# Big matmuls of a three-pass fp32 kernel take turns between two PSUM banks

## The chip, the cores and the metric

The kernel runs on one core of one Trainium2 chip. The metric is the device time of one execution in microseconds (us); lower is better. The kernel before takes 2294.41 us, the median of 3 runs (2293.33 to 2296.01).

## What is computed

Two transformer-like blocks follow each other on 256 tokens of width 2048, all in fp32:

```
hybrid_layer:  h = rmsnorm(x, g_mix) @ w_in                 # 2048 x 5728 columns in nine parts
               y_ssd = state-space scan of (xbc, dt), gated by z
               y_att = attention over the top 64 keys by an index score
               x = x + concat(y_ssd, y_att) @ w_out         # 2048 x 2048
               u = rmsnorm(x, g_mlp) @ w_up                 # 2048 x 8192
               x = x + square(relu(u)) @ w_down             # 8192 x 2048
second block:  h = rmsnorm(x, g0) @ fox_w_in                # 2048 x (3 * 2048 + 16)
               h = forget-gate attention, 16 heads, @ fox_w_out
               x = x + rmsnorm(h, g1)
               h = square(relu(rmsnorm(x, g2) @ mlp_w1)) @ mlp_w2
               x = x + rmsnorm(h, g3)
```

## The kernel before

Nearly all of the work is products of 256 tokens with weight matrices that come from HBM once. A matrix is worked through in **panels** of 2048 x 512 weights: 95 of them. A panel has four **chunks** `j` of 512 x 512 weights (1 MB), and a chunk has four **k-tiles** `kk` of 128 rows.

An fp32 product is made of three matmuls of a narrower float type. Each operand is split in a high and a low part: SyncE loads a chunk into `raw`, ScalarE rounds it into `wh` (L501), VectorE subtracts and writes `wl` (L942). Activations are kept split in the same way (`XH`, `XL`, or `hh`, `hl` for the hidden layer). TensorE adds high x high, high x low and low x high into PSUM.

There are two forms of panel, and in both a panel's result lies in two PSUM banks of 128 x 512 fp32, `acc[o_par][0]` and `acc[o_par][1]` (banks 0 and 1 for even panels' outputs, banks 2 and 3 for odd ones; the other four banks serve small side work):

- `rows`: tokens are the stationary operand (128 of them), weights are moving (512 columns). Token tile `t` has bank `t`. A k-tile is 2 token tiles x 3 matmuls (L1705, L1706, L1707), a chunk is 24 matmuls.
- `cols`: weights are stationary (128 features), tokens are moving (256 columns). Feature tile `f` of four has a half of bank `f // 2`. A k-tile is 4 feature tiles x 3 matmuls (L1720, L1722, L1723), a chunk is 48 matmuls.

```
for kk in range(4):
    for t in tokens:              # rows: three matmuls into one bank, then the other
        o = acc[o_par][t][:, :]
...
for kk in range(4):
    for f in range(4):            # cols: six matmuls into one bank, then the other
        o = acc[o_par][f // 2][:, TOK * (f % 2):TOK * (f % 2 + 1)]
```

The order of the work on TensorE is written out by hand: `panel` and `first_panel` call one of the two forms for each chunk, and between chunks a table (`MIX_AT`, `FOX_AT`) puts side work into the row: transposes, index scores, attention heads. A chunk waits once, at its start, for `lo_ready` (its `wl`). A panel waits once, at its start, in `acc_wait`, for both of its banks to be read out (`acc_freed`). The last matmul of a chunk raises `chunk_used`; SyncE's next load of the same buffer, and ScalarE and VectorE's reading of a finished panel, wait for that. The end of the kernel has another order: for the last two chunks `rows` is called with one token tile at a time (`tokens` of `[0]` for both chunks, then of `[1]` for both), so that the first tile can be finished while the second is computed. There 24 successive matmuls write one bank, and then 24 the other.

Of the kernel before, what the change touches and what calls it, by code (L numbers as in the profile page):

```python
# [18 lines left out]
P = 128  # L19
TOK = 256  # L20
# [41 lines left out]
def hybrid_then_fox(nc, x, g_mix, w_in, conv_w, conv_b, dt_bias, a_log, d_skip, g_ssd, g_q, g_k,  # L62
# [3 lines left out]
    with ctx:  # L66
# [3 lines left out]
        def sb(name, shape, dt=F32):  # L70
            return ctx.enter_context(nc.sbuf_tensor(name, shape, dt))
# [3 lines left out]
        XH = sb("XH", [P, KT, TOK], F32R)  # L75
        XL = sb("XL", [P, KT, TOK], F32R)
        wh = sb("wh", [P, 4, 4, 512], F32R)
# [29 lines left out]
        raw, wl = T["raw"], T["wl"]  # L107
# [58 lines left out]
        acc = [[bank[0], bank[1]], [bank[2], bank[3]]]  # L166
# [1522 lines left out]
        def _(pe):  # L1689
# [7 lines left out]
            def rows(b, j, o_par, first, last, k0, h=XH, l=XL, tokens=range(NT), used=chunk_used):  # L1697

                pe.wait_ge(lo_ready, 4 * b + j + 1)
                for kk in range(4):  # L1700
                    for t in tokens:
                        o = acc[o_par][t][:, :]
                        sh, sl = (z[:, k0 + kk, t * P:(t + 1) * P] for z in (h, l))
                        mh, ml = wh[:, j, kk, :], wl[:, j, kk, :]
                        pe.matmul(o, sh, mh, start=first and kk == 0, stop=False)  # L1705
                        pe.matmul(o, sh, ml, start=False, stop=False)  # L1706
                        mm = pe.matmul(o, sl, mh, start=False, stop=last and kk == 3)  # L1707
                if used is not None:
                    mm.then_inc(used, 1)

            def cols(b, j, o_par, first, last, k0):


                pe.wait_ge(lo_ready, 4 * b + j + 1)
                for kk in range(4):
                    for f in range(4):
                        o = acc[o_par][f // 2][:, TOK * (f % 2):TOK * (f % 2 + 1)]
                        sh, sl = (z[:, j, kk, f * P:(f + 1) * P] for z in (wh, wl))
                        mh, ml = XH[:, k0 + kk, :], XL[:, k0 + kk, :]
                        pe.matmul(o, sh, mh, start=first and kk == 0 and f % 2 == 0, stop=False,  # L1720
                                  skip_group_check=True)
                        pe.matmul(o, sh, ml, start=False, stop=False, skip_group_check=True)  # L1722
                        mm = pe.matmul(o, sl, mh, start=False, stop=last and kk == 3, skip_group_check=True)  # L1723
                mm.then_inc(chunk_used, 1)

            def turn_quarter(m, q):
# [30 lines left out]
            def panel(form, b, o, plan={}, slot=0):  # L1757
                acc_wait(o)
                for j in range(4):
                    if form is cols:  # L1760
                        cols(b, j, o % 2, j == 0, j == 3, 4 * j)
                    else:
                        rows(b, j, o % 2, j == 0, j == 3, 4 * j)
                    side_work(plan, slot + j)

            def mlp(m, b0, o0, u0):
                for half in range(2):
                    b, o, u = b0 + half * B_HALF, o0 + half * O_HALF, u0 + half * UP
                    if half == 0:
                        first_panel(cols, m, b, o)  # L1770
                    else:
                        panel(cols, b, o)
                    with pe.Fori(0, UP // 2 - 1) as i:
                        for s in (1, 2):
                            for k in range(2):
                                pe.wait_ge(acc_freed[(o + s) % 2][k], i + (o + s) // 2)
                            for j in range(4):
                                cols(b + 2 * i + s, j, (o + s) % 2, j == 0, j == 3, 4 * j)
                    panel(cols, b + UP - 1, o + UP - 1)
                    for n in range(DOWN):  # L1780
                        on = o + UP + n
                        acc_wait(on)
                        for j in range(8):
                            if n == 0:

                                pe.wait_ge(hl_ready, 2 * (u + j) + 4)
                            if m == 3 and half == 1 and n == DOWN - 1 and j > 5:
                                continue
                            rows(b + UP + 2 * n + j // 4, j % 4, on % 2, j == 0, j == 7, 4 * j, hh, hl)
                            if half == 1 and m == 1 and n > 0 and j == 3:  # L1790
                                turn_quarter(2, n - 1)
                if m == 3:

                    rows(B_END - 1, 2, on % 2, False, False, 24, hh, hl, [0], None)
                    rows(B_END - 1, 3, on % 2, False, True, 28, hh, hl, [0], first_tokens)
                    rows(B_END - 1, 2, on % 2, False, False, 24, hh, hl, [1])
                    rows(B_END - 1, 3, on % 2, False, True, 28, hh, hl, [1])
# [236 lines left out]
```

## Time and profile before

| | |
|---|---|
| median of 3 runs | 2294.41 us |
| profiled execution | 2293.16 us |
| its span | 2291.4 us |
| TensorE matmul busy | 2261.6 us (99%), 14211 instructions |
| TensorE weight load busy | 2024.1 us (88%) |
| VectorE busy | 1208.5 us (53%) |
| ScalarE busy | 946.4 us (41%) |
| DMA engines, mean | 55.7% by the weights' queue, 180 GB/s |
| mean granted TensorE clock | 0.998 |

The span is the time from the first to the last instruction of the profiled execution; 1.8 us lie around it. Matmuls are pipelined: one begins before the one ahead of it has ended, so the time of one is longer than its share of TensorE. What a matmul costs is the distance from its start to the next one's start, which the timeline gives, in steps of 0.01 us. Busy time above is the union of overlapping matmuls.

### The profile page before, as it was taken

Reading aid. Unit: us, or ns where it says so; the run is one execution under the profiler, and the core shown is the slowest. Engines: PE = TensorE matmul, PEld = TensorE weight load, DVE = VectorE, ACT = ScalarE, POOL = GpSimd, SP = SyncE. Lnnn points to the kernel's source line nnn. Section 1 sums busy time; section 2 is a strip of 40 time slices with the busy share of each in tenths; the row PEclk is TensorE's granted clock in tenths of the full one; section 3 lists DMA queues with packets and bytes.
Section 4 is the critical chain, followed back from the end, with each engine's and each line's share of the span. In section 5 each row is a group of like instructions: output and inputs, shape, how many; then the busy total and the mean of one; then the engine's idle time right before and its main releaser. Section 6 shows DMA issues by size and latency. Waiting matters only on the chain.

```text
span 2291.4 us, 32313 instructions
## 1 busy us (share of the span) xinstructions
PE 2261.6 (99%) x14211; PEld 2024.1 (88%) x14211; DVE 1208.5 (53%) x1167; ACT 946.4 (41%) x901; POOL 12.4 (1%) x34
## 2 busy tenths in 40 slices
PE   7999999999999999999999999999999999999998
PEld 7988778999988899988899987888998888999886
DVE  5688665545444354544455444555555443545444
ACT  5453564444433343434334434434435333434332
POOL 1000000000000000000000000000000000000000
PEclk9999999999999999999999999999999999999999
DMA  8445435666555666555555454555665556665554
GB/s 259 152 157 166 156 129 190 196 184 183 184 190 193 186 184 183 184 184 184 185 184 183 148 165 155 176 186 171 184 184 192 185 184 188 185 184 189 190 184 147
DMA packets 210908, 412.12 MB, mean 180 GB/s; under 512 B 12804, under 2 KB 12896, under 8 KB 210160
## 3 DMA queue, kind: packets, MB, share of 16 engines
q1 hardware_dynamic: 210368, 409.89, 55.7%
q8 instruction: 88, 1.44, 0.3%
q0 software_dynamic: 432, 0.62, 0.2%
q14 instruction: 20, 0.16, 0.0%
HBM read 408.39 MB, written 2.10 MB: 179 GB/s over the span
## 4 chain that ended last, share of the span: by engine, by line
PE 98%; DVE 1%; ACT 1%; DMA 0%; issue 0%; DVEq 0%; SPq 0%; ACTq 0%
PE bank L1705 16%; PE bank L1706 16%; PE bank L1707 16%; PE bank L1720 15%; PE bank L1723 15%; PE bank L1722 15%; PE bank L1803 1%; PE bank L1735 1%; PE bank L1828 0%; PE bank L1837 0%; PE bank L1922 0%; PE bank L1896 0%; PE bank L1815 0%; PE bank L1807 0%; PE bank L1829 0%; DMA G<-in_g_mix_dram 0%
## 5 line engine op out<-in xcount | busy, mean ns | idle before, releaser
L942 DVE TENSOR_TENSOR wl<-raw,wh 128x2048 fp32r<-128x2048 f32 x380 | 870.3, 2291 | 647.3 <-ACT wh L501 645.2
L501 ACT ACTIVATE wh<-raw 128x2048 fp32r<-128x2048 f32 x380 | 726.7, 1913 | 724.8 <-DMA raw<-in_mlp_w_dram 265.0
L1720 PE MATMUL bank<-XH,wh 128*128 128x256 f32 x2880 | 817.7, 284 | 0.2 <-issue 0.2
L1723 PE MATMUL bank<-XH,wl 128*128 128x256 f32 x2880 | 812.7, 282 | 0.0
L1722 PE MATMUL bank<-XL,wh 128*128 128x256 f32 x2880 | 810.3, 281 | 0.0
L1722 PEld LDWEIGHTS bank<-XL,wh 128*128 128x128 f32 x2880 | 547.2, 190 | 0.6 <-issue 0.5
L1720 PEld LDWEIGHTS bank<-XH,wh 128*128 128x128 f32 x2880 | 543.7, 189 | 3.7 <-issue 2.2
L1723 PEld LDWEIGHTS bank<-XH,wl 128*128 128x128 f32 x2880 | 542.8, 188 | 0.0
L1707 PE MATMUL bank<-wh,hl 128*128 128x512 f32 x1024 | 404.5, 395 | 0.0
L1706 PE MATMUL bank<-wl,hh 128*128 128x512 f32 x1024 | 404.4, 395 | 0.0
L1705 PE MATMUL bank<-wh,hh 128*128 128x512 f32 x1024 | 402.2, 393 | 0.0
L1706 PEld LDWEIGHTS bank<-wl,hh 128*128 128x128 f32 x1024 | 191.9, 187 | 47.0
L1705 PE MATMUL bank<-wh,XH 128*128 128x512 f32 x576 | 231.9, 403 | 1.3 <-DVE XL L950 1.3
L1705 PEld LDWEIGHTS bank<-wh,hh 128*128 128x128 f32 x1024 | 192.0, 188 | 45.5
L1707 PEld LDWEIGHTS bank<-wh,hl 128*128 128x128 f32 x1024 | 192.2, 188 | 44.1
L1706 PE MATMUL bank<-wl,XH 128*128 128x512 f32 x576 | 227.2, 394 | 0.0
L1707 PE MATMUL bank<-wh,XL 128*128 128x512 f32 x576 | 225.1, 391 | 0.0
L1098 DVE TENSOR_TENSOR RB<-RB 128x512 f32<-128x512 f32 x64 | 44.1, 689 | 244.8 <-ACT RB L594 244.8
L594 ACT ACTIVATE RB<-bank 128x512 f32<-128x512 f32 x64 | 38.1, 595 | 303.2 <-PE bank L1723 303.2
L1705 PEld LDWEIGHTS bank<-wh,XH 128*128 128x128 f32 x576 | 108.5, 188 | 26.1 <-issue 2.0
L1707 PEld LDWEIGHTS bank<-wh,XL 128*128 128x128 f32 x576 | 108.3, 188 | 26.0
L1706 PEld LDWEIGHTS bank<-wl,XH 128*128 128x128 f32 x576 | 108.0, 188 | 22.7 <-issue 0.5
(310 smaller groups left out, 819.7 us busy)
## 6 DMA issues: line engine op xcount, KB each, us to landing
raw<-in_mlp_w_dram SPq DMA_DIRECT2D x128, 1024.0 KB, 5.4
raw<-in_w_up_dram SPq DMA_DIRECT2D x64, 1024.0 KB, 5.5
raw<-in_w_down_dram SPq DMA_DIRECT2D x64, 1024.0 KB, 5.0
raw<-in_fox_w_in_dram SPq DMA_DIRECT2D x48, 1024.0 KB, 5.1
raw<-in_w_in_dram SPq DMA_DIRECT2D x44, 1024.0 KB, 5.0
raw<-in_w_out_dram SPq DMA_DIRECT2D x16, 1024.0 KB, 5.1
raw<-in_fox_w_out_dram SPq DMA_DIRECT2D x16, 1024.0 KB, 5.1
G<-in_norm_g_dram SPq DMA_DIRECT2D x4, 1024.0 KB, 5.9
```

The source lines that it names most:

```text
L501: act.activation(wh[:, j, :, :], raw[:, j, :, :], ACT.Copy).then_inc(hi_ready, 1)
L594: act.activation(RB[:, k, :], acc[o_par][k][:, :], ACT.Relu)\
L942: dve.tensor_tensor(wl[:, j, :, :], raw[:, j, :, :], wh[:, j, :, :].bitcast(F32), ALU.subtract)\
L1098: dve.tensor_tensor(RB[:, k, :], RB[:, k, :], RB[:, k, :], ALU.mult).then_inc(sq_ready, 1)
L1705: pe.matmul(o, sh, mh, start=first and kk == 0, stop=False)
L1706: pe.matmul(o, sh, ml, start=False, stop=False)
L1707: mm = pe.matmul(o, sl, mh, start=False, stop=last and kk == 3)
L1720: pe.matmul(o, sh, mh, start=first and kk == 0 and f % 2 == 0, stop=False, skip_group_check=True)
L1722: pe.matmul(o, sh, ml, start=False, stop=False, skip_group_check=True)
L1723: mm = pe.matmul(o, sl, mh, start=False, stop=last and kk == 3, skip_group_check=True)
L1735: mm = pe.transpose(bk[:, i * P:(i + 1) * P], src[:, t, k * P:(k + 1) * P], ident[:, :])
L1803: mm = pe.matmul(bk[:, ctr(t)], q[:, t * P:(t + 1) * P], k[:, 0:(t + 1) * P], start=True, stop=not a)
```

## The change

In `rows`, the loop over token tiles moves inside the loop over the three products, so successive matmuls write bank 0, 1, 0, 1. In `cols`, the four feature tiles are taken as two pairs `(0, 2)` and `(1, 3)`, each with one tile in either bank, and the pair is the innermost loop. For one output tile the three products and the k-tiles keep their order. `start`, which clears a bank's accumulation, stays on the first matmul that a panel makes in each bank.

```diff
                 for kk in range(4):
-                    for t in tokens:
-                        o = acc[o_par][t][:, :]
-                        sh, sl = (z[:, k0 + kk, t * P:(t + 1) * P] for z in (h, l))
-                        mh, ml = wh[:, j, kk, :], wl[:, j, kk, :]
-                        pe.matmul(o, sh, mh, start=first and kk == 0, stop=False)
-                        pe.matmul(o, sh, ml, start=False, stop=False)
-                        mm = pe.matmul(o, sl, mh, start=False, stop=last and kk == 3)
+                    mh, ml = wh[:, j, kk, :], wl[:, j, kk, :]
+                    for x, m in ((h, mh), (h, ml), (l, mh)):
+                        for t in tokens:
+                            mm = pe.matmul(acc[o_par][t][:, :], x[:, k0 + kk, t * P:(t + 1) * P], m,
+                                           start=first and kk == 0 and x is h and m is mh,
+                                           stop=last and kk == 3 and x is l)
...
                 for kk in range(4):
-                    for f in range(4):
-                        o = acc[o_par][f // 2][:, TOK * (f % 2):TOK * (f % 2 + 1)]
-                        sh, sl = (z[:, j, kk, f * P:(f + 1) * P] for z in (wh, wl))
-                        mh, ml = XH[:, k0 + kk, :], XL[:, k0 + kk, :]
-                        pe.matmul(o, sh, mh, start=first and kk == 0 and f % 2 == 0, stop=False,
-                                  skip_group_check=True)
-                        pe.matmul(o, sh, ml, start=False, stop=False, skip_group_check=True)
-                        mm = pe.matmul(o, sl, mh, start=False, stop=last and kk == 3, skip_group_check=True)
+                    mh, ml = XH[:, k0 + kk, :], XL[:, k0 + kk, :]
+                    for half in range(2):
+                        for w, m in ((wh, mh), (wh, ml), (wl, mh)):
+                            for f in (half, half + 2):
+                                mm = pe.matmul(acc[o_par][f // 2][:, TOK * (f % 2):TOK * (f % 2 + 1)],
+                                               w[:, j, kk, f * P:(f + 1) * P], m,
+                                               start=first and kk == 0 and half == 0 and w is wh and m is mh,
+                                               stop=last and kk == 3 and w is wl, skip_group_check=True)
```

How the order on TensorE moves is seen at two places. The first is a k-tile of the first `cols` chunk (out <- moving operand, stationary operand, and the moving shape). Before:

```order
L1720 MATMUL bank0<-XH,wh 128x256
L1722 MATMUL bank0<-XL,wh 128x256
L1723 MATMUL bank0<-XH,wl_50 128x256
L1720 MATMUL bank0<-XH,wh 128x256
L1722 MATMUL bank0<-XL,wh 128x256
L1723 MATMUL bank0<-XH,wl_50 128x256
L1720 MATMUL bank1<-XH,wh 128x256
L1722 MATMUL bank1<-XL,wh 128x256
L1723 MATMUL bank1<-XH,wl_50 128x256
```

Now, on TensorE at the same place:

```order
L1719 MATMUL bank0<-XH,wh 128x256
L1719 MATMUL bank1<-XH,wh 128x256
L1719 MATMUL bank0<-XL,wh 128x256
L1719 MATMUL bank1<-XL,wh 128x256
L1719 MATMUL bank0<-XH,wl_50 128x256
L1719 MATMUL bank1<-XH,wl_50 128x256
L1719 MATMUL bank0<-XH,wh 128x256
```

Where the bank changed after every sixth matmul, it changes after each. The second place is the start of a `rows` chunk of the first MLP's second layer. Before:

```order
L1705 MATMUL bank2<-wh,hh_97 128x512
L1706 MATMUL bank2<-wl_50,hh_97 128x512
L1707 MATMUL bank2<-wh,hl_98 128x512
L1705 MATMUL bank3<-wh,hh_97 128x512
L1706 MATMUL bank3<-wl_50,hh_97 128x512
L1707 MATMUL bank3<-wh,hl_98 128x512
L1705 MATMUL bank2<-wh,hh_97 128x512
```

Now, on TensorE at the same place:

```order
L1704 MATMUL bank2<-wh,hh_97 128x512
L1704 MATMUL bank3<-wh,hh_97 128x512
L1704 MATMUL bank2<-wl_50,hh_97 128x512
L1704 MATMUL bank3<-wl_50,hh_97 128x512
L1704 MATMUL bank2<-wh,hl_98 128x512
L1704 MATMUL bank3<-wh,hl_98 128x512
L1704 MATMUL bank2<-wh,hh_97 128x512
```

Where the bank changed after every third matmul, it changes after each. The orders of VectorE, ScalarE and SyncE are the same before and after, and TensorE issues as many matmuls. Where `rows` is called with one token tile, nothing moves.

## Rows read from the trace of the kernel before

**Rows 1.** The page: busy time of the engines, granted TensorE clock in 40 slices

```profile
PE 2261.6 (99%) x14211; PEld 2024.1 (88%) x14211; DVE 1208.5 (53%) x1167; ACT 946.4 (41%) x901; POOL 12.4 (1%) x34
...
PEclk9999999999999999999999999999999999999999
```

**Rows 2.** The page: the chain that ended last, by engine and by line

```profile
PE 98%; DVE 1%; ACT 1%; DMA 0%; issue 0%; DVEq 0%; SPq 0%; ACTq 0%
PE bank L1705 16%; PE bank L1706 16%; PE bank L1707 16%; PE bank L1720 15%; PE bank L1723 15%; PE bank L1722 15%; PE bank L1803 1%; PE bank L1735 1%; PE bank L1828 0%; PE bank L1837 0%; PE bank L1922 0%; PE bank L1896 0%; PE bank L1815 0%; PE bank L1807 0%; PE bank L1829 0%; DMA G<-in_g_mix_dram 0%
```

**Rows 3.** Waits of TensorE: total us, times, longest

```profile
PE bank L1735 <- DVE XN L974: 14.0, 2, 8.0
PE bank L1735 <- DVE HG L1643: 4.7, 1, 4.7
```

**Rows 4.** Groups of matmuls by shape: busy us, mean ns | idle before

```profile
L1720 PE MATMUL bank<-XH,wh 128*128 128x256 f32 x2880 | 817.7, 284 | 0.2 <-issue 0.2
L1723 PE MATMUL bank<-XH,wl 128*128 128x256 f32 x2880 | 812.7, 282 | 0.0
L1722 PE MATMUL bank<-XL,wh 128*128 128x256 f32 x2880 | 810.3, 281 | 0.0
...
L1706 PE MATMUL bank<-wl,hh 128*128 128x512 f32 x1024 | 404.4, 395 | 0.0
L1705 PE MATMUL bank<-wh,hh 128*128 128x512 f32 x1024 | 402.2, 393 | 0.0
L1705 PE MATMUL bank<-wh,XH 128*128 128x512 f32 x576 | 231.9, 403 | 1.3 <-DVE XL L950 1.3
```

**Rows 5.** Timeline of a cols chunk: start us, us; matmuls 1, 3, 4, 6, 7, 48

```profile
595.43 0.28 PE L1720 MATMUL bank<-XH,wh 128*128 128x256 f32 x1
...
595.67 0.28 PE L1723 MATMUL bank<-XH,wl 128*128 128x256 f32 x1
595.79 0.29 PE L1720 MATMUL bank<-XH,wh 128*128 128x256 f32 x1
...
596.03 0.28 PE L1723 MATMUL bank<-XH,wl 128*128 128x256 f32 x1
596.14 0.28 PE L1720 MATMUL bank<-XH,wh 128*128 128x256 f32 x1
...
601.03 0.28 PE L1723 MATMUL bank<-XH,wl 128*128 128x256 f32 x1
```

**Rows 6.** Timeline, 48 rows matmuls that change bank every third: first, last

```profile
2260.85 0.39 PE L1705 MATMUL bank<-wh,hh 128*128 128x512 f32 x1
...
2271.76 0.39 PE L1707 MATMUL bank<-wh,hl 128*128 128x512 f32 x1
```

**Rows 7.** Timeline, the kernel's last 48 matmuls, 24 in each bank: first, last

```profile
2272.00 0.39 PE L1705 MATMUL bank<-wh,hh 128*128 128x512 f32 x1
...
2282.91 0.40 PE L1707 MATMUL bank<-wh,hl 128*128 128x512 f32 x1
```

**Rows 8.** Timeline, 45 narrow matmuls of side work in one bank: first, last

```profile
66.14 0.28 PE L1859 MATMUL bank<-XH,NHm 128*96 128x256 f32 x1
...
71.28 0.28 PE L1861 MATMUL bank<-XH,NLm 128*96 128x256 f32 x1
```

**Rows 9.** Weight loads of cols: busy us, mean ns | idle before

```profile
L1722 PEld LDWEIGHTS bank<-XL,wh 128*128 128x128 f32 x2880 | 547.2, 190 | 0.6 <-issue 0.5
L1720 PEld LDWEIGHTS bank<-XH,wh 128*128 128x128 f32 x2880 | 543.7, 189 | 3.7 <-issue 2.2
```

**Rows 10.** Stretches after a wait of TensorE; the eighth column is the granted clock

```profile
1555.00:1556.00 1.00, 0.76 (x4) 0.76 (x5) 1.00 (x3) 0.00 (x0) 0.00 (x0) 0.50 0.28 107
1556.00:1559.50 3.50, 3.29 (x19) 3.08 (x18) 1.89 (x3) 2.85 (x3) 0.00 (x0) 0.67 0.00 0
```

**Rows 11.** Timeline, the program's second and sixth cols matmul

```profile
17.95 0.41 PE L1722 MATMUL bank<-XL,wh 128*128 128x256 f32 x1
...
18.81 0.35 PE L1723 MATMUL bank<-XH,wl 128*128 128x256 f32 x1
```

## The prediction

> **What bounds the kernel now.** The order of reading is: busy time, the chain, TensorE's waits, the groups, and then the timeline, because the groups can't price this change. TensorE is busy for 99% of the span, VectorE for 53% and ScalarE for 41%, at full granted clock in all slices [rows 1]. The chain that ended last is TensorE for 98%, and six lines, the three matmuls of `rows` and the three of `cols`, make 93 of these points [rows 2]. TensorE's own waits come to some 19 us in its two main rows [rows 3], both before transposes that follow a normalization, where no big matmul stands. So the time is the number of big matmuls times the distance between their starts, and a change of their order counts in full or not at all: nothing hides it, and nothing else is in line to take over soon.
>
> The groups give 281 to 284 ns for a matmul of 256 columns and 393 to 403 ns for one of 512 [rows 4]. The reader must not take these as prices: a matmul begins before the one ahead of it has ended. The distance of starts is the price. In a chunk of `cols`, 48 matmuls span 595.43 to 601.03, which is 5.60 us over 47 steps, 119.1 ns a step [rows 5]. In `rows`, 48 matmuls span 2260.85 to 2271.76, 10.91 us over 47 steps, 232.1 ns [rows 6]. There are 3 x 2880 = 8640 of the first kind [rows 4], and 3 x (1024 + 576) = 4800 of the second. 8640 x 0.1191 + 4800 x 0.2321 = 1029 + 1114 = 2143 us, 93.5% of the span of 2291.4 us, which agrees with the chain.
>
> **The change, part by part.** No instruction comes or goes on TensorE, and VectorE, ScalarE and SyncE keep their order. What changes is which matmul follows which.
>
> *Steps to another bank.* `cols` has 8640 / 48 = 180 chunks. Before, 8 steps in 48 go to the other bank, now all do: 40 x 180 = 7200 new ones. `rows` has 4800 / 24 = 200 chunks; two at the end are worked one bank at a time and stay. Before, 8 steps in 24 change bank, now all do: 16 x 198 = 3168 new ones. Together 10,368 steps inside a bank become steps between banks. What is one worth? The kernel before holds both kinds at the same shape. The 48 matmuls of [rows 6] change bank after every third one, 15 times in 47 steps. The 48 that follow, the kernel's last, write 24 times one bank and 24 times the other, one change in 47 steps, with the same three products and the same shapes, and they too span 10.91 us, from 2272.00 to 2282.91 [rows 7]. Fourteen steps inside a bank in place of steps between banks cost 0.00 us. So a step between banks is worth nothing, and I put this term at **0**. The timeline is rounded to 0.01 us, so the bound on either side is 0.01 / 14 = 0.7 ns a step, and 10,368 x 0.7 ns = **7.3 us either way**. For `cols` the price is carried over from `rows`; what its own rows say agrees as far as they go: the step from the third to the fourth matmul, in one bank, is 0.12 us, and that from the sixth to the seventh, between banks, 0.11 us, one rounding step apart [rows 5]. And 45 matmuls of 256 columns that all write one bank are 5.14 us over 44 steps, 116.8 ns [rows 8]: a bit shorter than in `cols`, where every sixth step changes bank. They have 96 stationary columns where `cols` has 128, so this is a near row, not the same shape; but a penalty for staying in a bank would have made them the longer ones.
>
> A rule of the Trainium skill speaks for a gain, and this trace weighs against its use. The page "TensorE: Matmul & The Clock Gate", in "Wait — 56ns, not 53.3ns?", has warm matmuls start every N / 2.4 GHz + 2.5 ns, which is 109 ns at 256 columns and 216 ns at 512; here they are 10 and 16 ns slower. If all that were the price of staying in a bank, the change would bring 7200 x 10 + 3168 x 16 ns = 123 us, an estimate by that page, and the faster rival below would end at 2171 us. The comparison of [rows 6] and [rows 7] says that the excess, whatever it is, doesn't hang on the bank.
>
> *Steps with the same weights.* Before, the second matmul of each three has the stationary operand of the first; now none has, except in the one-tile calls. TensorE loads the weights anew in either case: there are as many loads as matmuls [rows 1], and in `cols` the load for L1722, whose weights are already in, takes 190 ns against 189 ns for L1720 [rows 9]. Nothing is skipped today, so nothing is lost: **0**. Both loads are longer than a step of 119 ns, so they overlap one another, as before. The bound is in the rivals.
>
> *Steps with the same moving operand.* Before, one step in four of `cols` and one in six of `rows` keeps it, now about half do. The step from L1723 to L1720 keeps it and takes 0.12 and 0.11 us in [rows 5], the chunk's mean is 0.119: **0**, within what the rounding shows.
>
> *Waits.* A panel waits for both banks before its first matmul, so that the second bank is written sooner (second matmul in place of fourth or seventh) costs nothing. A chunk's last matmul still raises `chunk_used`, so the loads into `raw`, and the reading of a finished panel, start as before. Bank 0 gets its last product next to the end rather than three or six matmuls ahead, but nobody reads it sooner than bank 1. No engine has a new wait. If TensorE did get faster, ScalarE and VectorE, at 41 and 53%, would still follow.
>
> The sum is 0. The profiled execution took 2293.16 us, and would take 2293.2 us. The median of the runs stands 1.25 us above it, so the forecast is **2294.4 us**.
>
> **The rivals.** 0.2%, or 4.6 us, is about what a measurement of this kernel can tell from no change.
>
> *Faster: staying in a bank costs something that the end of the kernel doesn't show.* From 256 to 512 columns a step grows by 232.1 - 119.1 = 113.0 ns; taken off the 119.1 ns, that leaves 6.1 ns that don't depend on the columns. Were these the bank's turnaround, 10,368 x 6.1 ns = 63 us would go: 2231 us. It decides from 0.45 ns a step on. For it: the constant exists, and nothing in the trace names its cause. Against it: [rows 7] would then be 14 x 6.1 = 85 ns longer than [rows 6], and they are equal to 10 ns; the narrow matmuls in one bank would be longer, and are not. Chance 0.08, most of it for a small gain in `cols`, where the like comparison is missing.
>
> *Slower: the weights.* If a load of unchanged weights does save something, at the place where L1722 and L1706 follow L1720 and L1705, the new order loses it in 2880 + 1584 = 4464 steps. In the groups L1722 is 3 ns shorter than L1720 [rows 4]. 4464 x 3 ns = 13 us: 2308 us. It decides from 1.0 ns a step. Against it: in `rows` L1706, on unchanged weights, is 2 ns longer than L1705, L1723 on new weights is only 1 ns longer than L1722, and L1720's mean holds the first matmuls of the program, at 0.4 us and more. Chance 0.04.
>
> *Slower: the clock.* After the wait of 4.7 us the granted clock was 0.50, the level of 1.2 GHz, and 0.67 on average over the next 3.5 us [rows 10]; together some 3.3 us at the lower level. The slowest even stretch of `cols` steps is at the program's start, 0.86 us over four steps, 215 ns [rows 11], 96 ns over the usual. A fall of 3.3 us holds 15 such steps and costs 1.5 us; three are needed to be seen, and one in each of the 45 panels of `cols` would cost 68 us: 2362 us. It takes gaps that TensorE doesn't have between big matmuls, and the change makes none. Chance 0.02. The Trainium skill has it as a danger of just this kind of order, in the same page under "A second HAM failure mode: psum-queue depth-cycling": cycling through banks left the engine with small pauses between groups, and its clock went up and down. This trace disagrees as far as it goes: `rows` changes bank at every third matmul, and the clock stays at 9 tenths or more in every slice [rows 1].
>
> *The change doesn't do what it says* can be left out: the order above shows the banks taking turns.
>
> **How the numbers follow.** No change has 0.86, faster 0.08, slower 0.06 (0.04 + 0.02). The range takes the bounds of the first term, 2294.4 - 7.3 and 2294.4 + 7.3, and so 2287 to 2302 us; the runs' own scatter (2293.3 to 2296.0) lies inside. The rivals' own numbers are outside it, their small versions inside.
>
> **What would show it.** In the profile after, a chunk of `cols` should again span 5.60 us over 47 steps and one of `rows` 232.1 ns a step, now with the banks alternating; the kernel's last 48 matmuls, which are not touched, should again span 10.91 us, like those ahead of them. The weight loads stay at 189 ns, and the waits before the transposes at 14 and 4.7 us. Wrong would be a step of `rows` of 228 ns (two thirds of the steps lose 6.1 ns) with 232 ns left at the end (the faster rival), steps 1 ns or more longer with the loads unchanged in number (the weights), or slices with a clock below 9 (the clock).

## The result: slower by 0.3%, and the profile after

The changed kernel takes 2301.39 us, the median of 10 runs (2297.95 to 2304.01), against 2294.54 us for the kernel before (10 runs, 2292.99 to 2296.66). The ratio is 1.0029, with a 95% interval of 1.0021 to 1.0038. The profiled execution took 2303.71 us and its span is 2302.0 us, 10.6 us over that of before. The median lies inside the range that was forecast; "no change" was wrong.

The page of the kernel after, the lines that answer to [rows 1] and [rows 2]:

```profile
PE 2272.4 (99%) x14211; PEld 2033.6 (88%) x14211; DVE 1208.3 (52%) x1167; ACT 946.6 (41%) x901; POOL 12.4 (1%) x34
...
PEclk9999999999999999999999999999999999999999
...
PE 98%; DVE 1%; ACT 1%; DMA 0%; issue 0%; DVEq 0%; SPq 0%; ACTq 0%
```

Everything is as it was but TensorE's busy time, which is 10.8 us longer for matmuls and 9.5 us longer for weight loads. The same number of each runs; the waits before the transposes are those of [rows 3]:

```profile
PE bank L1734 <- DVE XN L974: 14.1, 2, 8.0
PE bank L1734 <- DVE HG L1643: 4.7, 1, 4.7
```

So the steps between matmuls got longer. A step that is 1 ns longer can't be read from rows rounded to 10 ns, but it can be counted: in a fixed stretch that holds nothing but `cols` matmuls, a slower pace shows as fewer of them. Each of the two MLPs computes its hidden layer in two halves, each with 32 chunks of `cols` and then `rows` on `hh`; so there are four such stretches. Windows of 160 us in them, of the kernel before; the columns are the stretch, its length, TensorE's busy time and number of matmuls, granted clock, DMA share and GB/s:

```profile
435.00:595.00 160.00, 160.00 (x1346) 1.00 0.61 184
797.00:957.00 160.00, 160.00 (x1347) 1.00 0.61 184
1583.00:1743.00 160.00, 160.00 (x1346) 1.00 0.61 184
1935.00:2095.00 160.00, 160.00 (x1346) 1.00 0.61 184
```

The same windows of the kernel after:

```profile
435.00:595.00 160.00, 160.00 (x1335) 1.00 0.60 182
797.00:957.00 160.00, 160.00 (x1336) 1.00 0.61 184
1583.00:1743.00 160.00, 160.00 (x1336) 1.00 0.61 182
1935.00:2095.00 160.00, 160.00 (x1336) 1.00 0.61 182
```

Ten or eleven in 1346 are missing, 0.8%, at full clock: a step takes 119.9 ns in place of 119.06 ns. (The window counts one or two matmuls that reach in from its edges.) The loss isn't spread evenly. The timeline after shows pairs of matmuls there, with 0.25 us from the pair on `wl` to the next and 0.23 us from that to the third:

```profile
820.30 0.40 PE L1719 MATMUL bank<-XH,wl 128*128 128x256 f32 x2
820.55 0.40 PE L1719 MATMUL bank<-XH,wh 128*128 128x256 f32 x2
820.78 0.40 PE L1719 MATMUL bank<-XL,wh 128*128 128x256 f32 x2
```

By the starts in nanoseconds, averaged over the second half's chunks, the step from the last matmul on `wl` to the first on the next pair of tiles takes 124 ns and the other five 118 to 121 ns, and the weight load for that first matmul takes 195 ns. Before, the mean step is at most 120 ns in every place of the order and the mean load at most 190 ns. Over the whole kernel this load's group now has a mean of 192 ns, where [rows 9] has 189:

```profile
L1719 PEld LDWEIGHTS bank<-XH,wh 128*128 128x128 f32 x2880 | 450.1, 192 | 4.3 <-issue 2.6
```

A sum over the starts of all matmuls, kind by kind and against before, says where the 10.5 us between the first and the last matmul are: `cols` +7.6 us, `rows` on `XH` and `XL` +3.0 us, `rows` on `hh` and `hl` +0.1 us, side work -0.2 us. Of these, 1.0 and 1.5 us lie in single long steps. The 1.0 us in `cols` are mostly at the program's start, where after has 12 steps at some 213 ns and before 4. The 1.5 us in `rows` on `XH` are one fall of the clock, to be seen in the windows of after and then of before:

```profile
321.20:324.40 3.20, 3.20 (x8) 0.50 0.00 0
```

```profile
321.20:324.40 3.20, 3.20 (x15) 1.00 0.00 0
```

Eight matmuls run there at half clock in place of 15, just after a wait of 1.3 us. Such a fall isn't part of the pace: it comes and goes between executions of one kernel (e8 has it and e2, the same kernel, doesn't), and the kernel before has in its own runs levels 1.5 us apart (near 2293.1, 2294.6 and 2296.2), which would fit such falls, though no trace of its higher levels was kept. But the change may make it more frequent. Besides after it is in five of the profiles below (e4, e7, e8, e11, e12), and all six have the change's rhythm of weight loads in `cols` (e8 with the old `rows`); three more profiles with that rhythm and the eight without it have no fall there. It is a part of why one profile says 10.6 us and the medians 6.9. What is left in this profile as the change's own is a pace: some 6.6 us in `cols` and 1.5 us in `rows` on `XH`.

### The profile page after: what moved, and what is told of

Read it like the earlier page. It is cut to its first block, busy times and chain, and to the rows that moved or that the text cites. A ratio compares the mean times of both kernels' runs of the same rounds, so it can differ in the third digit from the quotient of the medians.

```text
span 2302.0 us, 32313 instructions
## 1 busy us (share of the span) xinstructions
PE 2272.4 (99%) x14211; PEld 2033.6 (88%) x14211; DVE 1208.3 (52%) x1167; ACT 946.6 (41%) x901; POOL 12.4 (1%) x34
## 4 chain that ended last, share of the span: by engine, by line
PE 98%; DVE 1%; ACT 1%; DMA 0%; issue 0%; DVEq 0%; SPq 0%; ACTq 0%
PE bank L1704 48%; PE bank L1719 45%; PE bank L1802 1%; PE bank L1734 1%; PE bank L1827 0%; PE bank L1836 0%; PE bank L1921 0%; PE bank L1895 0%; PE bank L1814 0%; PE bank L1806 0%; PE bank L1828 0%; DMA G<-in_g_mix_dram 0%; PE bank L1843 0%; DVE X L1684 0%; PE bank L1859 0%; PE bank L1858 0%
## 5 line engine op out<-in xcount | busy, mean ns | idle before, releaser
L1719 PE MATMUL bank<-XH,wh 128*128 128x256 f32 x2880 | 581.5, 284 | 0.0
L1719 PE MATMUL bank<-XH,wl 128*128 128x256 f32 x2880 | 581.4, 285 | 0.0
L1719 PE MATMUL bank<-XL,wh 128*128 128x256 f32 x2880 | 577.5, 282 | 0.0
L1719 PEld LDWEIGHTS bank<-XH,wh 128*128 128x128 f32 x2880 | 450.1, 192 | 4.3 <-issue 2.6
L1719 PEld LDWEIGHTS bank<-XL,wh 128*128 128x128 f32 x2880 | 442.2, 189 | 0.0
L1719 PEld LDWEIGHTS bank<-XH,wl 128*128 128x128 f32 x2880 | 441.6, 188 | 0.0
L1704 PE MATMUL bank<-wh,hl 128*128 128x512 f32 x1024 | 323.8, 396 | 0.0
L1704 PE MATMUL bank<-wl,hh 128*128 128x512 f32 x1024 | 322.3, 395 | 0.0
L1704 PE MATMUL bank<-wh,hh 128*128 128x512 f32 x1024 | 320.4, 393 | 0.0
L1704 PE MATMUL bank<-wh,XH 128*128 128x512 f32 x576 | 184.3, 401 | 1.3 <-DVE XL L950 1.3
```

Of the source, the lines that this page charges most:

```text
L1704: mm = pe.matmul(acc[o_par][t][:, :], x[:, k0 + kk, t * P:(t + 1) * P], m, start=first and kk == 0 and x is h and m is mh, stop=last and k ...
L1719: mm = pe.matmul(acc[o_par][f // 2][:, TOK * (f % 2):TOK * (f % 2 + 1)], w[:, j, kk, f * P:(f + 1) * P], m, start=first and kk == 0 and ha ...
```

## The experiments

Two theories at first: the new **order of operands** costs the time, or the **turns between banks** do. In `cols` the runs with other orders than the change's use one loop, whose two expressions give for each of the 12 matmuls of a k-tile the feature tile `f` and the product `n`, and, where it is not that tile's own, the output tile `g`; `rows` has the like for 6 matmuls:

```python
for p in range(12):
    f, n = ...                  # before: p // 3, p % 3
    g = f                       # the change: p // 6 + 2 * (p % 2), p % 6 // 2
    w, m = ((wh, mh), (wh, ml), (wl, mh))[n]
    mm = pe.matmul(acc[o_par][g // 2][:, TOK * (g % 2):TOK * (g % 2 + 1)], w[:, j, kk, f * P:(f + 1) * P], m, ...)
```

**e1, e2: half of the change each.** The new `rows` with the old `cols`, and the reverse.

> The change in rows alone, cols as before. The trace of the changed kernel has its rows chunks of the MLP layers at the old pace and its cols chunks slower. Theory 'weights' (in cols, and only there, the weight load that opens a new pair of tiles is slower because of the new order of stationary and moving operands): no change, 2294 to 2296 us, rows steps 232 ns. Rival 'banks' (taking turns between banks costs something everywhere): +2 to +3 us, since rows have 3168 of the 10368 new bank steps.

> The change in cols alone, rows as before. Theory 'weights': the whole loss is here: cols steps of 119.9 instead of 119.05 ns, 8640 x 0.95 ns = +8 us, about 2302 us. Rival 'banks': about two thirds of the loss, +5 us.

e1 took 2297.26 us, ratio 1.0009 (0.9999 to 1.0018); e2 took 2297.31 us, ratio 1.0008 (0.9999 to 1.0018). The windows of e1, and then of e2:

```profile
797.00:957.00 160.00, 160.00 (x1346) 1.00 0.61 184
```

```profile
435.00:595.00 160.00, 160.00 (x1348) 1.00 0.61 184
797.00:957.00 160.00, 160.00 (x1348) 1.00 0.61 184
```

Both intervals reach down to no change, so the medians alone say little; the traces say more. e1's 2.3 us over the kernel before of its own round is what the theory 'banks' expected, but its trace has 1.46 us of it in `rows` on `XH`, nothing in `rows` on `hh`, which take 2016 of the 3168 new turns between banks, and its `cols` keep their pace. e2 fits neither theory. It has the new `cols`, and in the MLPs they are *faster* than before: 1348 in a window, 118.9 ns a step. Only 30 of its 180 chunks, in the projections, are at 119.9. (A chunk's pace is taken from the starts of its 7th and its 48th matmul.) On balance the pace costs e2 nothing: its `cols` steps, the single long ones left out, are 119.04 ns on average, as before. So the two halves don't add: the new `cols` order has two paces, and something about `rows` decides between them.

**e3, e4: banks alone, operands alone.** In `rows` and `cols`, a product no longer goes to the output tile of its own operands, so neither kernel computes the result; they are there for their time.

```diff
 # e3
+f, n = p // 3, p % 3                          # operands as before
+g = p // 6 + 2 * (p % 2)                      # banks as in the change
 # e4
+f, n = p // 6 + 2 * (p % 2), p % 6 // 2       # operands as in the change
+g = p // 3                                    # banks as before
```

> Operands in the order of the kernel before (the three products of a tile one after the other), but the matmuls write the banks in the order of the changed kernel, 0, 1, 0, 1; so products are added into the wrong tile, and the time alone is meant. Theory 'weights': time of the kernel before, 2294 to 2296 us, cols steps 119.05 ns, weight loads 189 ns at every position. Rival 'banks': the time of the changed kernel, about 2302 us, with one step in six of 123 to 124 ns.

> The opposite: operands in the order of the changed kernel, banks written in the order of the kernel before (three or six matmuls in a row to one bank), so products again go to the wrong tile. Theory 'weights': the time of the changed kernel, about 2302 us, with a load of 194 ns and a step of 123 to 124 ns at every sixth cols matmul. Rival 'banks': 2294 to 2296 us.

e3 took 2293.86 us, ratio 0.9998 (0.9989 to 1.0008); e4 took 2299.98 us, ratio 1.0021 (1.0011 to 1.0031). e3, then e4:

```profile
797.00:957.00 160.00, 160.00 (x1346) 1.00 0.61 184
...
1935.00:2095.00 160.00, 160.00 (x1347) 1.00 0.61 184
```

```profile
435.00:595.00 160.00, 160.00 (x1347) 1.00 0.60 183
797.00:957.00 160.00, 160.00 (x1336) 1.00 0.60 182
1583.00:1743.00 160.00, 160.00 (x1348) 1.00 0.61 184
1935.00:2095.00 160.00, 160.00 (x1336) 1.00 0.61 184
```

This settles the banks. With the turns of the change and the operands of before, the sum over the starts differs from before by 0.0 us in `rows`, and `cols` are 0.1 us shorter. The loss comes with the operands, and in e4 both paces stand side by side: two of the four halves at 1347 to 1348, two at 1336; 98 chunks are slow. In e4's second half the two signs of its expectation are there, every sixth step at 124 ns and the load for the next matmul at 195 ns; in e3's they are not.

**e5, e6: moving operands alone, stationary operands alone.** Banks as before. Stationary and moving tiles no longer belong together, so these two don't compute the result either.

```diff
 # e5
+f, n = p // 3, p % 3                          # stationary, as before
+f2, n2 = p // 6 + 2 * (p % 2), p % 6 // 2     # moving, as in the change
 # e6: the two exchanged
```

> Stationary operands and banks in the order of the kernel before, moving operands in the order of the changed kernel (each read twice in a row), in rows and cols; the pairs don't match, so products are wrong, and the time alone is meant. The profiles show that operand order, not bank order, carries the loss, that a cols chunk now runs at one of two paces, 118.9 or 119.9 ns a step, and that rows on XH and XL lose 0.8 ns a step. Theory 'weight loads' (the order in which stationary tiles are loaded decides): 2294 to 2296 us, cols at the old mixed pace of 119.05, no chunk at 119.9. Rival 'moving' (reading the same moving tile twice in a row decides): about 2300 us, many chunks at 119.9.

> The other half: stationary operands in the order of the changed kernel (two tiles in turn), moving operands and banks as before; products again wrong, the time alone is meant. Theory 'weight loads': about 2300 us, many cols chunks at 119.9 ns a step and rows on XH at +0.8 ns. Rival 'moving': 2294 to 2296 us.

e5 took 2295.78 us, ratio 1.0002 (0.9992 to 1.0011), e6 2296.24 us, ratio 1.0005 (0.9995 to 1.0014). The medians tell nothing apart; the traces do. Windows of e5, then of e6:

```profile
797.00:957.00 160.00, 160.00 (x1346) 1.00 0.61 184
```

```profile
797.00:957.00 160.00, 160.00 (x1349) 1.00 0.61 185
```

The stationary order puts `cols` on the two paces (e6: 118.9 ns in the MLPs, 30 chunks at 119.9 ns), the moving order doesn't (e5: no chunk at 119.9). But the moving order costs something in `rows` on `XH`. A run of 336 such matmuls without a break, its first and last rows, of before (to its end 1472.66 to 1550.58, 77.92 us):

```profile
1472.66 0.48 PE L1705 MATMUL bank<-wh,XH 128*128 128x512 f32 x1
...
1550.18 0.40 PE L1707 MATMUL bank<-wh,XL 128*128 128x512 f32 x1
```

of after (1479.88 to 1558.15, 78.27 us; the last row holds two):

```profile
1479.88 0.48 PE L1704 MATMUL bank<-wh,XH 128*128 128x512 f32 x1
...
1557.52 0.63 PE L1704 MATMUL bank<-wh,XL 128*128 128x512 f32 x2
```

and of e5 (1473.69 to 1551.97, 78.28 us):

```profile
1473.69 0.48 PE L1709 MATMUL bank<-wh,XH 128*128 128x512 f32 x1
...
1551.57 0.40 PE L1709 MATMUL bank<-wh,XL 128*128 128x512 f32 x1
```

Reading each moving tile twice in a row costs 0.35 us in 336 steps, 1 ns each; e6, without it, is at 77.92 us again, and over all `rows` on `XH` e5 loses 1.47 us, e6 0.0 us. So 'weight loads' held for `cols`, and 'moving' for `rows` on `XH`.

**e7, e8: the change, and its cols alone, once more.** For a second profile of each.

> The changed kernel itself once more, for a second profile. If the pace of a chunk is chosen by chance at the entry and then kept, the number of cols chunks at 119.9 ns differs from the 158 of 180 of the first profile, and the time with it, by 0.05 us a chunk. If it is fixed by the program, the same chunks are slow again.

> The change in cols alone once more: its first profile had 30 of 180 cols chunks at 119.9 ns and ran 2293.66 us, while its median was 2297.31. By chance at the entry: a number of slow chunks between 30 and 158, in step with the time. Fixed by the program: 30 again, with a time near 2294 us.

e7 took 2301.47 us and e8 2296.23 us (one execution each). The windows of e7:

```profile
435.00:595.00 160.00, 160.00 (x1347) 1.00 0.61 183
797.00:957.00 160.00, 160.00 (x1335) 1.00 0.60 182
1583.00:1743.00 160.00, 160.00 (x1348) 1.00 0.61 184
1935.00:2095.00 160.00, 160.00 (x1336) 1.00 0.61 184
```

The first profile had all four halves slow (158 chunks), this one the second and the fourth (98 chunks, the same as in e4). e8 has the 30 slow chunks of e2. So the pace of a half is settled within its first chunks and then kept, and it is partly chance. It isn't always the first chunk's: in the first profile the first half had three chunks at 118.9 ns before 29 at 119.9, and the third half one before 31. The first and third halves, which follow the norm's transposes, went either way; the others, which follow `rows` on `hh`, were slow in both profiles of the change and fast in both of its `cols` alone. They were fast in e6 too, where `rows` have the new stationary and the old moving order, and slow in e4, where they have both new. A half at the slow pace costs 32 x 48 x 1.0 ns = 1.5 us over the fast one.

**e9 to e12: what in the order does it, and what picks the pace.** The new `rows` are in e9 to e11. New theories for the order: the loads never repeat a tile; they jump by two tiles; two tiles take turns.

```diff
 # e9, neighbours (0, 1), (2, 3) in turn
+f, n = 2 * (p // 6) + p % 2, p % 6 // 2
 # e10, one tile at a time, wh wl wh
+f, n = p // 3, (0, 2, 1)[p % 3]
 # e11, wh0 wh0 wh2 wh2 wl0 wl2
+f, n = p // 6 + 2 * (0, 0, 1, 1, 0, 1)[p % 6], (0, 1, 0, 1, 2, 2)[p % 6]
 # e12, the new cols; rows in the new order only on hh and hl
+if h is XH:
+    ...
```

> The changed rows; in cols pairs of neighbouring tiles (0, 1) and (2, 3), both in one bank, in place of (0, 2) and (1, 3), products outside as in the change. Computes the reference. The runs so far show that the order of stationary tiles makes cols chunks lock to 118.9 or 119.9 ns a step. Theory 'no repeat' (it matters that no weight tile is loaded twice in a row, not which tile comes between): chunks at 118.9 and 119.9 again, many of them slow, 2299 to 2302 us. Rival 'distance' (it matters that the loads jump by two tiles, 1 KB in a partition): the old mixed pace of 119.06, about 2297 us with the 1.5 us of the changed rows.

> The changed rows; in cols one tile at a time as before, but its products in the order wh*XH, wl*XH, wh*XL, so that no weight tile is loaded twice in a row and no other tile comes between. Computes the reference up to the order of the sums. Theory 'no repeat': chunks lock to 118.9 or 119.9, 2299 to 2302 us. Rival 'alternation' (two feature tiles in turn is what matters): the old mixed pace of 119.06, about 2297 us.

> The changed rows; in cols pairs (0, 2) and (1, 3), but wh of a tile is loaded twice in a row as before: wh0 wh0 wh2 wh2 wl0 wl2. Computes the reference. Theory 'no repeat': old mixed pace of 119.06, about 2297 us. Rival 'alternation': chunks at 118.9 and 119.9, 2299 to 2302 us.

> The changed cols, and the changed rows only where they run on hh and hl (the MLPs' second layers); rows on XH and XL as before. The changed cols alone had 30 of 180 chunks at 119.9 in both profiles, the whole change 158 and about 98, although the rows on hh cost the same in either order. Theory 'entry' (the rows that a stretch of cols chunks follows decide at which of two paces it locks): the MLPs' cols chunks are slow in part as in the whole change, 80 or more slow chunks and 2297 to 2300 us. Rival 'XH rows' (the earlier rows on XH, or their 1.4 us, make the difference): 30 slow chunks, about 2296 us.

| run | median us | ratio to before | slow chunks of 180 |
|---|---|---|---|
| e9 | 2299.73 | 1.0020 (1.0010 to 1.0030) | 99 |
| e10 | 2295.46 | 1.0005 (0.9996 to 1.0015) | 0 |
| e11 | 2302.12 | 1.0027 (1.0017 to 1.0037) | 129 |
| e12 | 2299.50 | 1.0022 (1.0013 to 1.0032) | 128 |

Two windows each of e9, e10, e11, and then all four of e12:

```profile
797.00:957.00 160.00, 160.00 (x1336) 1.00 0.60 182
...
1935.00:2095.00 160.00, 160.00 (x1336) 1.00 0.61 182
```

```profile
797.00:957.00 160.00, 160.00 (x1346) 1.00 0.61 186
...
1935.00:2095.00 160.00, 160.00 (x1346) 1.00 0.61 184
```

```profile
797.00:957.00 160.00, 160.00 (x1336) 1.00 0.60 182
...
1935.00:2095.00 160.00, 160.00 (x1335) 1.00 0.60 181
```

```profile
435.00:595.00 160.00, 160.00 (x1347) 1.00 0.61 183
797.00:957.00 160.00, 160.00 (x1336) 1.00 0.60 182
1583.00:1743.00 160.00, 160.00 (x1335) 1.00 0.61 184
1935.00:2095.00 160.00, 160.00 (x1335) 1.00 0.61 184
```

e9 refutes the jump. e10 refutes "no repeat", which was also the mechanism of my rival on the weights: no tile is loaded twice in a row, and the pace is the old one; and e11 keeps the repeats and is as slow as the change. Alternation is left, or something that e9 and e11 share with the change and e10 doesn't: four loads from `wh` and then two from `wl`. e12 confirms the entry: `rows` on `hh` in the new order, themselves no slower, turn the halves that follow them, the second and the fourth, from e2's 1348 to 1336 and 1335; the third, which goes by chance, is slow here too.

**e13, e14: turns of two tiles, or the rhythm of the two weight buffers.** Again with the new `rows`.

```diff
 # e13: wh0 wh2 wl0 wh0 wh2 wl2
+f, n = p // 6 + 2 * (0, 1, 0, 0, 1, 1)[p % 6], (0, 0, 2, 1, 1, 2)[p % 6]
 # e14: each product over all four tiles
+f, n = (0, 2, 1, 3)[p % 4], p // 4
```

> The changed rows; in cols tiles and banks mostly take turns, but the loads come from the two weight buffers in the old rhythm of high, high, low: (wh0,XH) (wh2,XH) (wl0,XH) (wh0,XL) (wh2,XL) (wl2,XH). Computes the reference up to the order of the sums. So far every order with four loads from wh and then two from wl has chunks locked at 118.9 and 119.9 ns, and the orders with a rhythm of three have none. Theory 'rhythm of the buffers': no chunk at 119.9, pace 119.0 to 119.1, about 2296 us. Rival 'alternation' (two tiles in turn): 98 to 158 chunks at 119.9, 2299 to 2302 us.

> The changed rows; in cols each product runs over all four tiles, banks in turn: eight loads from wh, then four from wl. Computes the reference. Theory 'rhythm of the buffers': chunks locked again at some pace of their own (a rhythm of twelve), not the mixed pace of 119.06; if like the rhythm of six, 2297 to 2302 us. Rival 'alternation': here tiles never come back within a product and no two are in turn, so the mixed pace of 119.06 and about 2296 us.

e13 took 2295.45 us, ratio 1.0006 (0.9996 to 1.0016), e14 2294.76 us, ratio 1.0001 (0.9992 to 1.0011). e13, then e14:

```profile
797.00:957.00 160.00, 160.00 (x1347) 1.00 0.60 184
```

```profile
797.00:957.00 160.00, 160.00 (x1348) 1.00 0.61 184
...
1935.00:2095.00 160.00, 160.00 (x1348) 1.00 0.61 184
```

e13 mostly keeps the turns and has the old rhythm of high, high, low, and the old pace, with no slow chunk: the rhythm decides, not the turns. What it is about the rhythm isn't separated: its length of six, or that loads from `wl` stand side by side, which they do in every order that locks and in none that doesn't. e14, eight high and four low, is locked too, in all but a few chunks at 118.9 ns, and never at 119.9.

**e15: the version that the runs point to.** `cols` as in e14, `rows` as before.

> cols with each product over all four tiles, banks in turn (every chunk locked at 118.9 ns in the run before this one), rows in the order of the kernel before (which spares the 1.4 us that reading each moving tile twice in a row cost on XH). Theory 'rhythm of the buffers': cols lose 8640 x 0.13 ns = 1.1 us against the kernel before, rows nothing, about 2293.3 us against 2294.4; too small to be told by the medians, but the trace's cols steps should be 118.9 in every chunk whatever the rows. Rival 'entry' (rows in the old order bring in the slow pace): chunks at 119.9 or above, 2296 us and more.

It took 2293.77 us (11 runs), ratio 0.9998 (0.9989 to 1.0007). Its windows hold 1348 matmuls in all four halves, so the pace is fast whatever the rows before, but the 1.1 us that this is worth can't be told from no change, and the profile had more than that in single long steps. No version beats the kernel before.

## Why the prediction was wrong

*Steps to another bank: right.* The term was 0, and e3, which makes the same 10,368 new bank steps and changes nothing else, measures 0.1 us where the bound was 7.3 us. The comparison of [rows 6] and [rows 7] was the right one, because it holds the rhythm of the stationary operands fixed. Its bound was too narrow: each span is the difference of two rounded starts, so two spans can differ by 0.02 us unseen, which is 1.4 ns a step and 15 us. The weighing of the Trainium skill's figure ("TensorE: Matmul & The Clock Gate", "Wait — 56ns, not 53.3ns?") also stands: `cols` steps stay 10 ns over it in every order of banks tried.

*Steps with the same weights: this step failed.* I put the term at 0 because a load of unchanged weights takes as long as any [rows 9]. That still holds in `cols`, where an order that only removes the repeats costs nothing (e10). But I priced a sequence as a sum of single steps. What was changed with the repeats is the rhythm in which loads come from `wh` and `wl`, and that sets a pace for the whole stretch: 119.06 ns for the old rhythm of three, 118.9 or 119.9 ns for four and two. Together with the new `rows` the term was between +3.5 us (e7) and +6.6 us (the first profile); with the old `rows` (e2) it was about 0, so the price of the new `cols` also hangs on what runs ahead of them. Nothing in the trace before had that rhythm, so its price wanted a bound of its own; the only one given, 13 us, stood with the rival on the weights at a chance of 0.04.

*Steps with the same moving operand: this failed too, by less.* Put at 0 from two steps read at 10 ns; it measured +1.5 us, 1 ns a step in `rows` on `XH`, nothing in `rows` on `hh`, and nothing of its own in `cols`.

*Waits, other engines, clock: right.* The waits of [rows 3] are unchanged. The rival on the clock, for which the Trainium skill spoke ("TensorE: Matmul & The Clock Gate", "A second HAM failure mode: psum-queue depth-cycling"), didn't come: the clock is 1.00 in the windows of the slow pace, and banks in turn alone (e3) changed nothing. The clock did fall once more in after than before, but behind a wait.

*The rivals.* The faster one fell with e3. The slower one on the weights had the right operand and the wrong mechanism. The sign that I named, a chunk of `cols` at 5.60 us over 47 steps, would be 5.64 us at the slow pace; that is a difference that the timeline can just show, but 0.04 us in 180 chunks is all of the loss in `cols`. The other sign, steps 1 ns or more longer with as many loads, came at 0.9 ns. My chance of 0.86 for no change rested on one term being well bounded, and two others were given no bound in the sum. That the median fell inside the range is luck: the range was the bound on the banks, which cost nothing.

*How far it is settled.* Shown: banks cost nothing; the stationary order carries the loss in `cols`, the moving order that in `rows` on `XH`; seven kernels with the rhythm of four and two have slow chunks (30 to 158), six with a rhythm of three have none, nor have the two with eight and four; the order of `rows` on `hh` has a part in which pace the next half takes. Open: which part of the chip sets these paces; how the entry picks one; why reading a weight tile twice in a row costs something when the stationary tiles come from `XH` and nothing when they come from `hh`; whether the new order makes falls of the clock more frequent.

## What to carry to other kernels

An order of operands is not priced step by step: where an engine is busy for 99% of the time, a repeating sequence of loads can lock at a pace of its own, and 0.9 ns in 119 was 0.3% of this kernel. Count instructions in a long window when the steps are below the timeline's rounding, and bound every property that a reordering changes (banks, stationary, moving), each with a stretch in which it alone differs. To find out which of them costs, give up the pairing of products and output tiles: a kernel that is timed only can have the banks of one order and the operands of the other.

## What the runs showed that I had not expected

The pace of one instruction sequence had two stable values, 118.9 and 119.9 ns, with full granted clock in both. A stretch of 32 chunks and some 180 us kept the one that it had taken within its first four chunks, over more than a hundred k-tiles and a wait on a semaphore at each chunk. In the same program different executions had different ones (windows of after and of e7), which moves the time by 1.5 us a stretch; that is as large as a fall of the clock. Both together could make up the 6 us over which the changed kernel's runs scatter, but only two of its executions were traced.
